# Gate tiles of branch A: from the merge into the attention, with two shifts in the order of the projections

## The reference, cut to what matters

```python
h = rmsnorm(x, norm_g)
aq, ak, av, az, buv, bz, cq, ck, cv, cz, gl = split_cols(h @ w_in)
ya = rmsnorm(diff_attention(rope(aq), rope(ak), av, lam)) * (1 - lam_init) * silu(az)
yb = u * (w_causal @ layernorm(vb) + sgu_b) * silu(bz)      # u, vb = gelu(buv)
yc = dilated_attention(rope(cq), rope(ck), cv) * silu(cz)
pb = [y @ w for y, w in zip((ya, yb, yc), w_branch)]        # three times 1024 x 1024
merged = sum(sigmoid(gl[n]) * pb[n] for n in range(3))      # gl[n]: 1024 columns of h @ w_in
return x + merged @ w_out
```

## Time and profile before

| | |
|---|---|
| median of 3 runs | 4192.47 us |
| the profiled execution, its time | 4189.5 us |
| its span, first to last instruction | 4187.8 us |
| TensorE, VectorE, ScalarE, GpSimd busy | 90%, 41%, 30%, 26% |
| mean granted TensorE clock | 0.955 |
| DMA: moved, mean rate | 243.92 MB, 58 GB/s |

### The profile page before, as it was taken

How to read it: one execution, slowest core, us unless ns; L and a number is a source line. 1 busy time by engine, 2 the same in 40 slices (tenths; PEclk the granted TensorE clock), 3 DMA queues, 4 the chain that set the end, 5 groups by cost and what they waited for, 6 DMA issues and landing times.

```text
span 4187.8 us, 51192 instructions
## 1 busy us (share of the span) xinstructions
PE 3778.1 (90%) x20820; PEld 3328.4 (79%) x20820; DVE 1726.9 (41%) x3180; ACT 1270.3 (30%) x2868; POOL 1106.8 (26%) x819
## 2 busy tenths in 40 slices
PE   5999998999999799998899999778988997988898
PEld 4877777788878578777778887668978997888898
DVE  6523554433343550455343334443333334333333
ACT  3212443133331220344223342122244412234441
POOL 2632222312223362222232222325200033420011
PEclk9999999999999899999999999879999998999998
DMA  2111011311133112110221113121100031110012
GB/s 109 36 61 66 33 48 41 136 36 41 39 112 126 51 41 76 51 46 31 79 98 41 41 36 136 61 82 60 42 21 14 20 122 50 43 50 12 12 40 91
DMA packets 81740, 243.92 MB, mean 58 GB/s; under 512 B 10336, under 2 KB 21856, under 8 KB 81504
## 3 DMA queue, kind: packets, MB, share of 16 engines
q1 hardware_dynamic: 81504, 240.64, 16.6%
HBM read 190.07 MB, written 50.53 MB: 57 GB/s over the span
## 4 chain that ended last, share of the span: by engine, by line
PE 70%; DVE 14%; ACT 8%; issue 6%; POOL 2%; DMA 1%; SPq 0%; DVEq 0%; POOLq 0%; ACTq 0%
PE pj L1139 49%; PE po L1343 4%; PE po L1234 4%; PE pS L1323 3%; PE pS L1325 2%; PE pS L1205 1%; DVE KK L1969 1%; DVE tmp L1957 1%; PE pS L1206 1%; PE pt L1221 1%; ACT PT L1736 1%; PE pj L1309 1%; ACT PT L1532 1%; DVE tmp L1960 1%; DVE tmp L1954 1%
## 5 line engine op out<-in xcount | busy, mean ns | idle before, releaser
L1139 PE MATMUL pj<-Hhi,Whi 128*128 128x512 f32 x2432 | 971.1, 399 | 76.3 <-DVE Hlo L1839 23.6
L1139 PE MATMUL pj<-Hhi,Wlo 128*128 128x512 f32 x2432 | 956.2, 393 | 0.0
L1139 PE MATMUL pj<-Hlo,Whi 128*128 128x512 f32 x2432 | 955.5, 393 | 0.0
L2396 POOL TENSOR_SCALAR Whi<-stage 128x1024 fp32r<-128x1024 f32 (+4 forms) x272 | 274.3, 1008 | 2267.7 <-DMA stage<-wstream 1314.1
L2398 POOL TENSOR_TENSOR Wlo<-stage,Whi 128x1024 fp32r<-128x1024 f32 (+4 forms) x272 | 619.9, 2279 | 22.7
L1139 PEld LDWEIGHTS pj<-Hhi,Whi 128*128 128x128 f32 x2432 | 462.3, 190 | 181.4 <-issue 29.2
L1139 PEld LDWEIGHTS pj<-Hhi,Wlo 128*128 128x128 f32 x2432 | 461.6, 190 | 99.2
L1139 PEld LDWEIGHTS pj<-Hlo,Whi 128*128 128x128 f32 x2432 | 462.5, 190 | 92.8
L1139 PE MATMUL pj<-H2hi,Whi 128*128 128x348 f32 (+1 forms) x864 | 292.7, 339 | 70.3 <-ACT Fx L1577 20.7
L1139 PE MATMUL pj<-H2lo,Whi 128*128 128x348 f32 (+1 forms) x864 | 289.4, 335 | 0.0
L1139 PE MATMUL pj<-H2hi,Wlo 128*128 128x348 f32 (+1 forms) x864 | 288.9, 334 | 0.0
(11 more groups left out here) (301 smaller groups left out, 6303.2 us busy)
## 6 DMA issues: line engine op xcount, KB each, us to landing
stage<-wstream SPq DMA_DIRECT2D x228, 512.0 KB, 4.2
merged<-Mb SPq DMA_DIRECT2D x32, 512.0 KB, 2.9
Mb<-merged SPq DMA_DIRECT2D x32, 512.0 KB, 4.1
gates<-tmp SPq DMA_DIRECT2D x48, 256.0 KB, 2.2
TH<-gates SPq DMA_DIRECT2D x24, 512.0 KB, 5.3
xres<-X SPq DMA_DIRECT2D x16, 520.0 KB, 5.5
xr<-xres SPq DMA_DIRECT2D x16, 520.0 KB, 4.6
X<-xT SPq DMA_DIRECT2D x8, 512.0 KB, 6.7
```

The costliest lines, as they stand in the source:

```text
L1139: x = pe.e.matmul(ps, w[a][:, u.koff + k * P:u.koff + k * P + P], moving(u.of, b, k, u.t0, u.n), start=k == 0 and i == 0, stop=k == u.K - ...
L2396: pool.e.tensor_scalar(upper, stage, 1.0, 0.0, ALU.mult, ALU.add).then_inc(*pool.tick("whi", c))
```

## The change

All eight gate tiles of branch A are stored ones, two in each head, as in branch C; `merge` of branch 0 computes none. In branch A, at a head's first step, one filler is put between the scores and the turning. In the mixing stage the blocks 5, 6 and 7 get one filler each, and three follow the last `lnmix`.

```diff
-SHARE = {"a": (1, 1, 1, 1), "c": (2, 2, 2, 2)}
-DIRECT = {0: (1, 3, 5, 7), 1: range(8), 2: ()}
+SHARE = (2, 2, 2, 2)
+DIRECT = {0: (), 1: range(8), 2: ()}
...
-            for _ in range(2):
+            for _ in range(2 if n < 5 else 1):
                 self.fill()
                 self.aside()
...
-        share = SHARE[br]
         for s, (j, qb) in enumerate(steps):
             more = s + 1 < len(steps)
             if qb == 0:
-                z, g = z_units(j), gates[2 * sum(share[0:j]):2 * sum(share[0:j + 1])]
+                z, g = z_units(j), gates[2 * sum(SHARE[0:j]):2 * sum(SHARE[0:j + 1])]
...
             if more:
                 scores(s + 1)
+            if diff and qb == 0:
+                self.fill(1)
             turns(s)
```

## The result

The changed kernel takes 4247.66 us (median of 4 runs, 4242.48 to 4250.29); the kernel before, run beside it, 4191.23 us (4 runs). The ratio is 1.0133, 95% interval [1.0116, 1.0151]: slower by 56 us. The forecast was 4236 us, slower by 43.4, with a range of 4213 to 4260. The direction was right, and so was the mechanism in merge 0 and in the mixing stage; in the attention one of the terms, the gain at block 6, did not come. The loss was 13 us larger than the sum.

A forecast was written before the change was run, and what follows sets the result against it. TensorE, busy 90%, bounds the kernel. Attention +35.1, merge 0 -21.7 and mixing +8.3 make +21.7 us a layer, +43.4 for two; on 4192.5 that gives 4236 us, range 4213 to 4260.

The forecast's parts named there:

- the gain at block 6: Branch A attention: rotations start 1.6 us earlier, so the 4.5 us wait shrinks by 1.6; three heads, -4.9 us.
- Part 2, merge 0: Merge 0: gate projections leave, the store-load-gating loop sets a period of 8.65 us; -21.7 us a layer (-26.3 to -13.7).
- the landing of the gate load: Merge 0: added gate load lands at 732.8, near the lower end of 732.4 to 734.1, giving an 8.4 us period.
- Rival B: Merge 0: waits bring the low clock, TensorE bounds at 10.25 us a tile, only -10.5 us; 4258 us, chance 0.09.
- Rival E: Merge 0: transfers stay hidden, -43 us, stores 5.6 us apart; needs loads ahead of stores; 4193 us, chance 0.05.
- Part 1, attention: Branch A attention: +43.6 us of gate projections less 8.5 covered, +35.1 us a layer (+11.9 to +43.6).
- the waits of block 5: Branch A attention, head 3: waits of 1.47 and 0.85 us at block 5 go, -2.3 us.
- Rival F: Attention: four GpSimd weight splits a layer each hold a waited-for VectorE instruction 2.3 us, +9.2 a layer; 4254 us, chance 0.05.
- One more at block 6 ahead of the queries and keys: Attention, heads 0 to 2: a gate projection there lets rotations start on time; -4.9 us for three heads.
- The 1.25 us that the early projection covers: Attention, first turning of head 0: TensorE's wait for the difference of the softmaxes is covered, -1.25 us.
- Part 3, mixing: Mixing stage: new waits of 3.7, 2.1 and 1.7 us, the wait behind `yb` stays; +8.3 us a layer (-2.4 to 11.3).
- rival C: Mixing stage: the three tail projections cover the wait of `yb`, -2.4 us instead; 4214 us, chance 0.10.

The follow-up runs named there:

- gates_ahead: Kernel before with all branch A gates in the attention, no early projection or mixing edit, and merge loads of tile d+1 issued before tile d's store: 4146.02 us, 0.9903.
- split_early: Changed kernel, but SyncE stores the half gate tile of block 6 only behind the first query projection: 4242.08 us, ratio 1.0130 to before.
- mix_only: Kernel before with the mixing edit alone (one filler each at norms 5 to 7, three behind): 4208.20 us, ratio 1.0050.
- gates_only: Kernel before with branch A's gates moved into the attention, no early projection and no mixing edit: 4194.31 us, ratio 1.0014.
- early_h0: Changed kernel with the early projection in head 0 alone: 4223.33 us, ratio 1.0088 to before.
- after_bare5: Changed kernel, but heads 0 to 2 get no projection at query block 5; the early projection stays: 4231.35 us, ratio 1.0107 to before.

## Why the prediction was right, and what its sum missed

**The frame held.** Work was taken from a stage in which TensorE never waited into one where it waited at places that the projections don't cover. The measured loss, 56.4, lies in the range; 13 us are missing in the sum, and all three parts erred in the same direction.

**Part 2, merge 0: right in form, one term too small.** The first store comes 763.51 - 754.83 = 8.7 us behind the last transpose (forecast 717.5 - 708.87 = 8.6), and gating and additions take the 2.77 us that the forecast had as 2.75. The mis-sized term is the landing of the gate load. I took it at 732.8, 4.8 us behind its issue and near the lower end of the bounds 4.4 and 6.1, and 0.25 more for a late sum; in the seven periods VectorE could start 5.0 to 6.5 us behind the issue, 5.5 in the mean. These loads run beside stores, sum loads and weight loads at a DMA share of 0.53: the middle of the two bounds would have been nearer than the lower end. Period 9.14 against 8.65, seven times: 3.4 us a layer. Rival B (low clock) was partly there, 0.88 in the stage, and hidden behind the chain: TensorE waited anyway. Rival E came true exactly when its condition was made: with the loads ahead, the stores are 5.5 us apart, and gates_ahead's merge 0 is the 47.4 us that E worked out as 44.7 + 2.8.

**Part 1, attention: near the number, with the main gain wrong.** "The wait shrinks by 1.6 us" at block 6 failed, and with it 4.9 of the 8.5 us that were to be covered. VectorE did start its rotations in time, but GpSimd's split moved from the subtraction ahead of them onto the first of them and took the gain. Nor would a gain have come off the 4.53 us wait at once. The rotation of the first key projection releases the scores, that of the second stands ahead of the output scaling; as long as TensorE waits for the first, an earlier start comes off that wait: in head 0 it was 0.65 us before, 0.99 after and 0.33 in split_early, each time with 4.53 behind it. At head 3 the waits of block 5 went, but others grew (0.78 to 1.21 us at a later output transpose), so its gain was smaller than 2.3. In all the stage's idle time fell by 1.7 us and not by 8.5.

On the other side its busy time grew by 353.72 - 315.34 = 38.4 us and not by 43.6, at a granted clock of 0.97 against 0.95. That made good 5.2 of the 6.8 us, by luck: nothing in the sum stood for it, and it isn't shown to come from the change, for mix_only has the clock of 0.97 with the attention of before, and against it the busy time grew by 43.1. How much of it was scatter of one execution stays open; by these traces the sum was low by 1.5 to 6 us a layer. Rival F had the lock right and its effect wrong: the change added no collision to the rotations of a head, it moved one.

**What the sum didn't see.** It costed the change as it stood and never asked what each of its edits did against the others. "One more at block 6 ahead of the queries and keys" was costed by what it covers, and not against where the same projection would have stood without the early one. Without it the two left over fall behind the rotations, at blocks 6 and 7, halve the long wait, and the clock stays up: +6 us for the kernel without the mixing edit, and not +37. The 1.25 us that the early projection covers was costed; the 31 us of two layers that it costs were not.

**Part 3, mixing: right.** The waits were 4.24, 0.47 and 1.61 us, 6.3 in all (forecast 3.7, 2.1 and 1.7, 7.5); `yb` did start behind the tail, and its wait stayed (rival C is out). TensorE resumed 10.55 us later and not 8.3: the low clock behind the first wait, 0.52 over 5.6 us, some 3 us, was charged in the bound (11.3) and not in the sum. At the first store of merge 1 the loss is 9.3, since part of the low clock behind `yb` (0.51 before, 0.71 after, each over 6.3 us) is given back. mix_only confirms the form: +20.2 for two layers, 10.1 each, with the same three waits.

## What to carry to other kernels

When filler work has fixed slots, a filler placed earlier is taken from a later slot: cost the slot that it leaves, and above all the one behind the burst that loads another engine (here four rotations on VectorE), not only the wait that it covers. Before work is moved out of a stage that never waits, find the chain that the work hides; if it is a store followed by a dependent load on one queue, issue the next loads before the store, and the same move turns from +6 us into -43. When several small edits come as one change, cost each against the kernel with the others.

## What was not expected of the hardware

- **Length of a wait and the clock behind it.** In branch A, layer 0, the 4.53 us waits were followed by a granted clock of 0.68 to 0.82 over the next 8 us in after, and of 0.61 to 0.76 in before. Those of 2.35 us were followed by 1.00 at the three places of gates_only, two of early_h0 and the first of after_bare5, but by 0.79 at the other two of after_bare5 (at 576.08 and 671.32, with 1.00 over the 6 to 10 us before them). The 2.61 us wait of head 3 is followed by 0.50 over 8 us in before and by 0.79 in after. So neither the length of the wait nor the code behind it alone tells it. The clock was 2.5 of the 5.7 us that a head lost; what else decides it, no run here shows.
- **A 128x512 instruction of a rotation takes 0.68 us alone and 1.4 to 2.8 us** beside GpSimd's split of a weight tile, and the 128x1024 subtraction 1.28 and up to 3.44. In the heads of layer 0 looked at (before, after, split_early) the slow one is the one that meets the split, so a split that comes later is paid by another instruction, and a late step on VectorE can itself be the mark of one.
- **512 KB loads behind a 512 KB store on the same queue** let VectorE start 5.0 to 6.5 us after their issue (3.4 for the first, with no store ahead). In gates_ahead the same transfers run at a DMA share of 0.82 (289 GB/s), and TensorE idles 0.4 us in the whole of merge 0, since the issues are a tile ahead.
